# Recurrent levels of a hybrid decoder step: products first, then the masked copies, the next level's decays last

## The reference

```python
b = jnp.cumsum(lc, axis=1)                                    # lc: log of the forget gates
dec = jnp.exp(jnp.where(tri, b[:, :, None] - b[:, None, :], -jnp.inf))
att = jnp.einsum('bthk,bshk,btshk->bhts', qc, kc, dec)
o = jnp.einsum('bthk,bhkv->bthv', qc * jnp.exp(b), S) + jnp.einsum('bhts,bshv->bthv', att, vc)
```

## Time and profile before

| | |
|---|---|
| median of 3 runs | 2084.98 us (2084.07 to 2086.77) |
| profiled execution | 2084.28 us, span 2082.5 us |
| TensorE busy | 2033.7 us, 98% |
| VectorE busy | 1208.2 us, 58% |
| ScalarE busy | 703.3 us, 34% |
| GpSimd busy | 277.9 us, 13% |
| granted TensorE clock, mean | 0.994 |

### The profile page before, as it was taken

The page is one execution under the profiler, slowest core; times in us unless marked ns, Lnnn a source line. Parts: engine busy times, 40 slices in busy tenths (PEclk is TensorE's granted clock), DMA queues, the critical chain, the costliest instruction groups (busy, mean ns, idle before and its releaser), DMA issues.

```text
span 2082.5 us, 37424 instructions
## 1 busy us (share of the span) xinstructions
PE 2033.7 (98%) x15293; PEld 1845.5 (89%) x15293; DVE 1208.2 (58%) x2019; ACT 703.3 (34%) x1097; POOL 277.9 (13%) x262
## 2 busy tenths in 40 slices
PE   9999999999999999999999999999999999999998
PEld 7766897789889999999997677679988999999998
DVE  5477477775354666246636699674444566525653
ACT  5344444523323222122234425443232332212223
POOL 1022004521001000000014256320000100000000
PEclk9999999999999999999999999999999999999999
DMA  6488223533542222222224225643443222222222
GB/s 214 140 268 305 94 75 109 172 95 131 205 155 74 81 82 82 82 87 86 72 78 143 57 81 195 216 122 102 152 172 137 82 82 81 92 82 82 82 76 76
DMA packets 221757, 249.80 MB, mean 120 GB/s; under 512 B 18594, under 2 KB 175660, under 8 KB 221382
## 3 DMA queue, kind: packets, MB, share of 16 engines
q1 hardware_dynamic: 200774, 200.40, 30.2%
q0 software_dynamic: 9872, 28.65, 4.2%
q10 hardware_dynamic: 10940, 18.35, 2.7%
HBM read 234.15 MB, written 13.00 MB: 119 GB/s over the span
## 4 chain that ended last, share of the span: by engine, by line
PE 88%; DVE 6%; ACT 2%; issue 1%; DMA 1%; PEld 1%; PEldq 0%; ACTq 0%; SPq 0%; POOL 0%; DVEq 0%
PE PS L931 57%; PE PS L909 9%; PE PS L997 6%; PE PS L1418 1%; PE PS L1436 1%; PE PS L1794 1%; PE PS L1775 1%; PE PS L1447 1%; PE PS L1847 1%; PE PS L1091 1%; PE PS L1459 1%; DVE stat L2875 1%; PE PS L1116 1%; PE PS L1278 1%; PE PS L1674 1%
## 5 line engine op out<-in xcount | busy, mean ns | idle before, releaser
L931 PE MATMUL PS<-xr_r,WH 128*128 128x256 f32 (+1 forms) x1920 | 569.3, 296 | 0.0
L931 PE MATMUL PS<-hT_r,WH 128*128 128x320 f32 (+1 forms) x1856 | 551.2, 297 | 2.2 <-DVE W_r L2698 1.6
L931 PE MATMUL PS<-hT_r,W_r 128*128 128x320 f32 (+1 forms) x1856 | 549.3, 296 | 0.0
L2698 DVE TENSOR_TENSOR W_r<-W,WH 128x1024 fp32r<-128x1024 f32 (+1 forms) x219 | 280.2, 1302 | 325.1 <-ACT WH L1944 324.7
L931 PE MATMUL PS<-arena_r,WH 128*128 128x320 f32 (+1 forms) x1840 | 419.3, 296 | 0.0
L1944 ACT ACTIVATE WH<-W 128x1024 fp32r<-128x1024 f32 (+1 forms) x262 | 266.4, 1034 | 437.2 <-PE PS L931 290.4
L931 PEld LDWEIGHTS PS<-xr_r,WH 128*128 128x128 f32 x1920 | 364.6, 190 | 0.7 <-issue 0.7
L931 PEld LDWEIGHTS PS<-hT_r,WH 128*128 128x128 f32 x1856 | 352.5, 190 | 2.9 <-issue 2.1
L931 PEld LDWEIGHTS PS<-hT_r,W_r 128*128 128x128 f32 x1856 | 352.4, 190 | 0.0
L931 PEld LDWEIGHTS PS<-arena_r,WH 128*128 128x128 f32 x1840 | 312.0, 190 | 0.1
L931 PE MATMUL PS<-arena_r,W_r 128*128 128x320 f32 (+1 forms) x664 | 196.5, 296 | 0.0
(11 more groups left out here) (477 smaller groups left out, 3072.5 us busy)
## 6 DMA issues: line engine op xcount, KB each, us to landing
W<-in_w_ffn_in SPq DMA_DIRECT2D x176, 256.0 KB, 3.3
W<-in_w_ffn_out SPq DMA_DIRECT2D x40, 512.0 KB, 3.4
W<-in_w_in_ab SPq DMA_DIRECT2D x28, 512.0 KB, 3.7
C<-in_cache_mem_k SPq DMA_DIRECT2D x10, 1024.0 KB, 9.1
C<-in_cache_diff_k POOLq DMA_DIRECT2D x32, 256.0 KB, 4.4
C<-in_cache_diff_k SPq DMA_DIRECT2D x32, 256.0 KB, 4.2
W<-in_w_xk SPq DMA_DIRECT2D x16, 512.0 KB, 3.6
W<-in_w_xv SPq DMA_DIRECT2D x16, 512.0 KB, 4.2
```

The source lines that it names most:

```text
L931: ins = mm(o, w[:, k, c * 128:c * 128 + 128], v(k0 + k)[:, t0:t1], start=opens and first and k == 0 and e == 0, stop=last and k == nk - 1 ...
L2698: v_.tensor_tensor(slot_view(WL, NW, n), slot_view(W, NW, n), plain(slot_view(WH, NV, n)), ALU.subtract).then_inc(lo_done, 1)
```

## The change

The last lines of the loop body are put in another order. Level n's products come first, then the masked copies of level n-1, and then the decays of level n+1. The loop now gives P(2), A(1), D(3), P(3), A(2), D(4), and so on to P(6), A(5), D(7), P(7), A(6). What the instructions compute and which semaphores they wait for is as before, and no other engine's list is changed.

```diff
             for n in range(2, len(LEVELS)):
+                product(n)
+                attend_level(n - 1, LEVELS[n - 1])
                 if n + 1 < len(LEVELS):
                     decays(n + 1)
-                product(n)
-                attend_level(n - 1, LEVELS[n - 1])
```

## The result

The changed kernel takes 2094.45 us (median of 6 runs, 2091.23 to 2096.10) against 2084.60 us before (6 runs). That is 9.9 us slower by the medians. The ratio of the runs is 1.0040, with a 95% interval of 1.0030 to 1.0051, which is 6.3 to 10.6 us. The profiled execution has a span of 2092.6 us, 10.1 more than before. The forecast was 2098.0, in a range of 2089 to 2102.

The account below looks back on a forecast made before the run. TensorE, busy 98% of the span, was taken as the bound. Terms of -1.9, +3.8, +1.7, +4.2, +4.4 and +0.8 us gave +13.0, so 2084.98 became 2098.0 us, range 2089 to 2102.

Parts of the forecast that it names:

- part (a): On VectorE, level 2's product no longer stands behind level 3's decays, which removes TensorE's 1.9 us wait.
- Part (b): On VectorE and ScalarE, decays, exponential, product, copies form one closed ring of 9.1 to 10.1 us, without room for GpSimd splits.
- Part (c): ScalarE's two copies of a memory block, behind a late exponential, free their PSUM bank late; waits of 3.8 and 4.2 us.
- slot 8: Memory-projection weight slot on TensorE that could start at 380.5; waits 4.2 us for ScalarE's memory copies.
- slot 4: Memory-projection weight slot on TensorE; starts at 359.4 instead of 355.6 after level 3's late decays; wait 3.8 us.
- level 4: TensorE's level 4 matmuls could start at 375.3 but wait 1.7 us for the product ending at 377.0.
- level 7: TensorE's level 7 matmuls could start at 407.1 but wait 4.4 us for the product ending at 411.4.
- lower clock: TensorE's clock after the new waits; taken as adding 0, worked out as 0 to 0.8 us, up to 4 in the range.
- the closest call: Level 3's decays on VectorE at 349.8 against GpSimd's split at 349.5; split assumed first, otherwise the total is +10.7 us.
- Rival 1: Not slower: few collisions, level 2's wait goes and nothing takes its place; 2083.1 us, chance 0.08.
- Rival 2: VectorE's two halves stay together, so a step meets one split, not two; +0.9 us, 2085.9, chance 0.06.
- Rival 3: The closed VectorE and ScalarE ring binds, with half the collisions; +6 us, 2091, the foot of the forecast's own case.

Follow-up runs that it names:

- e7: Kernel before, with only level 2's product moved ahead of level 3's decays; 2082.70 us, ratio to before 0.9984.
- e2: Changed kernel, with GpSimd filling the low weight part with zeros instead of computing splits for this stage's 16 memory slots; 2082.28 us, ratio to before 0.9982.
- e3: Changed kernel's loop reordered to products, next level's decays, then masked copies, splits kept; 2082.72 us, ratio to before 0.9985.
- e4: Changed kernel, with ScalarE's two copies of a memory block ahead of the exponentials of levels 3 and 5; 2093.24 us, ratio to before 1.0039.
- e8: Changed kernel plus an unused maximum over 1024 columns on VectorE ahead of level 3's decays, some 1.1 us; 2097.88 us, ratio to before 1.0057.
- e5: The changed kernel measured again, unaltered; 2094.60 us, ratio to before 1.0050.
- e6: Changed kernel plus an unused maximum over 256 columns on VectorE ahead of level 3's decays, some 0.3 us; 2095.41 us, ratio to before 1.0050.

## Why the prediction was right

**What bounds it, and part (a).** Right. Level 2 starts at 351.26; 351.27 was forecast, by 1.9 us in place of the 2.2 of the list of waits. In e7, with P(2) alone put ahead, the whole stage gains 2.0 us, and no other order or fill here gains more.

**Part (b), the ring.** Right, with both of its conditions: e2 has the ring without the collisions and loses nothing, e3 has the splits without the ring and loses nothing, the changed kernel has both.

**Part (c), the copies behind the exponential.** Right at slot 8 (3.83 us of idle time measured, a wait of 4.2 forecast), and e4 takes that wait away by moving the copies. At slot 4 there was no wait in the changed kernel, where 3.8 was forecast.

**The terms.**

| | forecast | measured |
|---|---|---|
| level 2 | -1.9 | -1.9 |
| slot 4 | +3.8 | 0.0 |
| level 4 | +1.7 | +1.8 |
| slot 8 | +4.2 | +4.1 |
| level 7 | +4.4 | +4.3 |
| the end of the stage | +0.8 | +0.9 |
| lower clock | 0 | +2.1 |
| stage | +13.0 | +11.2 |
| given back behind it | 0 | -1.1 |

Each measured figure is the difference between the two timelines from one step's start to the next (1.58 at slots 8 and 9 and 0.5 at the end make the clock's 2.1; the last 0.1 is rounding). Two terms were wrong, 3.8 too much and 2.1 too little, and they partly hide each other; that the total came out within 2 us of the stage's is partly luck. The first is slot 4: "The split of 349.5 is first: D(3)'s halves end at 353.0 and, behind the split of 352.3, at 356.6". D(3) was issued at 349.42 and ended at 352.02. The prediction named this as the closest call, with +10.7 for the other outcome, but took the wrong side. It ended 0.02 us behind the 352 that the prediction had named as a sign of being wrong, so that sign stood on the edge. The prediction also read more into the two collisions before than they held: a waiting split does not always go ahead of VectorE's next instruction. In e8, where it does, the wait is there with 3.7 us. But there level 4's wait is missing, so the two waits of the forecast stood together in no run, and the close match of level 4's term (1.7 and 1.8), forecast for a start 3.8 us later, is in part luck too. The second is the clock: "The first two losses would be hidden", and "I take 0". Two falls came. The last cost 0.5 us, within the 0 to 0.8 that the prediction had worked out for it. The one in the middle, which was said to be hidden, was not: E(6) at 389.29 stood behind the cast that slot 9 releases, not behind D(6), which was done at 387.3. e5, with that fall elsewhere, is 1.6 us shorter. The Trainium skill's warning (TensorE: Matmul & The Clock Gate, HAM oscillation — how this bites in real kernels) would have put the stage at +13.8, and with D(3) on the right side at 11.5 (the 10.7 of its other outcome and 0.8). The traces agree with it in kind: in the changed kernel two idle times of about 4 us have a fall behind each, and in e8 all three have one (0.70 at 358 to 361 us, 0.75 at 385 to 388, 0.50 at 413 to 417). Idle times of about 2 us went either way: the 2.03 before level 4 has a fall behind it in e5 and none in the changed kernel.

**The rivals.** Rival 1 needed D(3) done by 352.1. It was done at 352.02, and the rest of the ring still met splits: the point named as deciding did not decide. Rival 2, halves that stay together, is what D(3) itself did, but P(2), D(4), P(4), D(7) and P(7) each had a split of the weights between their halves. Rival 3 (+6) was too low.

## What to carry to other kernels

Before moving a step in an in-order engine's list, write down the ring that it belongs to: the step, what another engine makes of its result, and the later step that waits for that. The work that stands between the two steps hides the other engine's time; taken out from there, it leaves the ring closed and without slack. Where GpSimd computes on two SBUF operands beside VectorE, a reordering also moves every step against those instructions, and each meeting costs up to the whole of the other's (2.3 us here), so count the meetings and not only the busy times. When one wait is to be removed, hoist the one step that is late (e7), and leave the order that hides the rest.

## What the runs showed of the hardware beyond that

GpSimd's fill (0.95 us, writing only) ran beside VectorE's two-operand instructions without lengthening them (1.35 us). When both engines issue within some tenths of a microsecond, the order need not be that of issue: in e6 a split issued 0.22 us ahead of D(3) waited for both of its halves, 2.7 us in all. In e5's D(6) one issued 0.16 us behind a first half went ahead of the second (3.40 us). These distances rest on the start times that the profile gives for GpSimd, which are rough. What decides between these cases is open.
